# First mixer's attentions: later copies and values, the sink as a column of the softmax rows, one reciprocal for two units

## The reference, cut to what matters

```python
def swa_branch(q, k, v, sinks):            # 6 heads, window of 128, blocks of 128 queries
    scores = einsum(q, k) * (A_DH ** -0.5) # each block of queries against its own block of keys and the one before
    scores = where(valid, scores + alibi, -inf)
    probs = softmax(concatenate([scores, sink], axis=-1), axis=-1)[..., :-1]
    return einsum(probs, v)

def stickbreak_branch(q, k, v):            # 4 heads, blocks of 128 queries against all keys before them
    log_keep = where(strict, log_sigmoid(-z), 0.0)
    suffix = cumsum(log_keep, reverse=True) - log_keep
    a = where(strict, exp(log_sigmoid(z) + suffix), 0.0)
    return einsum(a, v)
```

## Time and profile before

| | us |
|---|---|
| median of three runs | 3040.37 |
| lowest and highest run | 3039.09, 3042.96 |
| profiled execution | 3033.97 |
| its span, first to last instruction | 3032.2 |
| softmax half, from the third pair's scores on (22 pairs) | 58.74 |
| stick half, seven pairs with filled-in products | 38.62 |
| stick half, eight pairs without | 60.54 |
| from the last pair's scores to the barrier | 26.43 |

### The profile page before, as it was taken

The page is one execution under the profiler, slowest core; times in us unless marked ns, Lnnn a source line. Parts: engine busy times, 40 slices in busy tenths (PEclk is TensorE's granted clock), DMA queues, the critical chain, the costliest instruction groups (busy, mean ns, idle before and its releaser), DMA issues.

```text
span 3032.2 us, 39599 instructions
## 1 busy us (share of the span) xinstructions
PE 2841.1 (94%) x15451; PEld 2339.6 (77%) x15451; DVE 2033.7 (67%) x3470; ACT 1163.3 (38%) x1969; POOL 82.3 (3%) x152
## 2 busy tenths in 40 slices
PE   3999999688999998899999999989989999999999
PEld 3878885466888887678888888868757788888887
DVE  5444317768445556558777778779985877777875
ACT  3234227534225555434333334431134433333444
POOL 1000000210130000000000000000000000000000
PEclk7999999898998999799999999999989999999999
DMA  8110200024100000223333274311101333335632
GB/s 310 29 32 22 63 28 10 5 85 126 42 18 1 1 1 1 91 97 111 112 111 111 84 282 142 97 48 47 36 16 63 105 112 111 111 111 194 217 96 102
DMA packets 185700, 256.28 MB, mean 85 GB/s; under 512 B 29575, under 2 KB 138539, under 8 KB 181035
## 3 DMA queue, kind: packets, MB, share of 16 engines
q1 hardware_dynamic: 181520, 232.45, 23.3%
q10 hardware_dynamic: 3995, 21.30, 1.7%
HBM read 186.62 MB, written 67.11 MB: 84 GB/s over the span
## 4 chain that ended last, share of the span: by engine, by line
PE 67%; DVE 8%; ACT 1%; issue 1%; DMA 0%; DVEq 0%; ACTq 0%
PE ps L1567 27%; PE ps L1575 14%; PE ps L1522 10%; PE ps L1470 4%; PE ps L1380 3%; PE ps L1452 2%; PE ps L1434 2%; PE ps L1631 2%; PE ps L1122 1%; PE ps L1682 1%; PE ps L1001 1%; PE ps L1668 0%; DVE ht L2836 0%; PE ps L1358 0%; PE ps L1428 0%
## 5 line engine op out<-in xcount | busy, mean ns | idle before, releaser
L1567 PE MATMUL ps<-x_ops,w_ring 128*128 128x512 f32 x3696 | 840.3, 389 | 6.3 <-ACT even_rows L2185 3.2
L1567 PEld LDWEIGHTS ps<-x_ops,w_ring 128*128 128x128 f32 x3696 | 693.1, 188 | 151.6 <-issue 7.9
L1575 PE MATMUL ps<-a_ring,w_ring 128*128 128x512 f32 x1848 | 419.7, 389 | 0.0
L1575 PEld LDWEIGHTS ps<-a_ring,w_ring 128*128 128x128 f32 x1848 | 346.7, 188 | 72.6 <-DVE w_ring L2925 0.7
L1522 PE MATMUL ps<-h_high,ring_parts 128*128 128x512 f32 x1024 | 320.6, 394 | 18.0 <-DVE h_low L2409 9.3
L2127 ACT ACTIVATE w_ring<-ring 128x512 fp32r<-128x512 f32 x230 | 144.2, 629 | 300.6 <-PE ps L1567 284.8
L1522 PEld LDWEIGHTS ps<-h_high,ring_parts 128*128 128x128 f32 x1024 | 193.5, 190 | 63.7 <-issue 13.5
L2418 DVE TENSOR_TENSOR ring_parts<-ring,ring_parts 128x1024 fp32r<-128x1024 f32 (+2 forms) x77 | 91.7, 1192 | 210.1 <-ACT ring_parts L1769 209.5
L1522 PE MATMUL ps<-h_low,ring_parts 128*128 128x512 f32 x512 | 200.7, 392 | 0.0
L2925 DVE TENSOR_TENSOR w_ring<-ring,w_ring 128x512 fp32r<-128x512 f32 x230 | 157.6, 685 | 38.8 <-ACT w_ring L2127 38.8
L1769 ACT ACTIVATE ring_parts<-ring 128x1024 fp32r<-128x1024 f32 (+2 forms) x77 | 76.0, 989 | 275.7 <-PE ps L1522 177.2
(11 more groups left out here) (476 smaller groups left out, 4637.2 us busy)
## 6 DMA issues: line engine op xcount, KB each, us to landing
a_raw<-act_kept SPq DMA_DIRECT2D x70, 512.0 KB, 3.8
act_kept<-even_rows SPq DMA_DIRECT2D x12, 1536.0 KB, 5.1
act_kept<-odd_rows SPq DMA_DIRECT2D x10, 1536.0 KB, 5.1
ring<-in_ffn_w_gate_dram SPq DMA_DIRECT2D x12, 1024.0 KB, 5.8
ring<-in_ffn_w_up_dram SPq DMA_DIRECT2D x12, 1024.0 KB, 6.0
ring<-in_conv_w_pw_dram SPq DMA_DIRECT2D x24, 512.0 KB, 3.9
late<-in_ffn_w_gate_dram SPq DMA_DIRECT2D x10, 1024.0 KB, 5.8
late<-in_ffn_w_up_dram SPq DMA_DIRECT2D x10, 1024.0 KB, 6.1
```

The costliest lines, as they stand in the source:

```text
L1567: last = mm(o, w_ring[:, i % 4, wp_, P * k:P * k + P], x_ops[:, X_OP[p], rp_, k, :], start=p in "176" and k == 0 and p_ == 0, stop=k == 3 ...
L1575: last = mm(bank(OUT_BANK[DOWN_GROUP[p] + c_]), w_ring[:, (A_UNITS + b) % 4, wp_, P * c_:P * c_ + P], a_ring[:, b % 4, rp_, :], start=p in ...
```

## The change

It touches the one stage. (1) The softmax rows get an input place of their own (`soft_in`, six rows of 260 columns, one per head in the units' order) and an output place (`soft_out`, eight rows). Column 256 of an input row holds the head's sink, negated, written once ahead of the loop. The exponential reads 257 columns and its sum has the sink in it; the sink's own exponential and DVE's sum go. (2) DVE finishes two units at once: after the biases of n and n+1 it waits for the exponentials of n-2 and n-1, takes one reciprocal of two columns and multiplies two rows. (3) `TURN_LAG` becomes `COPY_LAG` = 3 on ACT, and on PE the step of n has the transposes of n-3, the values of n-6 and n-5, and the transposes of n-2. (4) The wait for a free row goes from the biases and, for units 48 and 49, from the sigmoids; `row_freed` is n-3 from unit 52 on and 47 for units 50 and 51.

```diff
-        soft_rows = part(14336, (4 * S,))
+        soft_in = part(14336, (A_H, 260))
+        soft_out = part(14336 + A_H * 260, (8, 260))
...
-        TURN_LAG, OUT_LAG = 4, 7
+        COPY_LAG, VALUE_LAG, OUT_LAG = 3, 6, 7
...
-                return soft_rows[:, 256 * (n % 16):256 * (n % 16) + 256]
+                return soft_out[:, n % 8, 256 - first_units[n].w:256]
...
-            if n < N_SWA:
-                return n - 15
-            return N_SWA - 16 + 4 * (n - N_SWA + 1) if n < N_SWA + 4 else n - 3
+            return n - 3 if n >= N_SWA + 4 else N_SWA - 1
...
-            for n in range(0, N_FIRST + TURN_LAG + 2, 2):
+            for n in range(0, N_FIRST + VALUE_LAG, 2):
                 if n < N_FIRST:
                     scores_pair(n)
                 for m in range(ym_at(n), min(3 * 2 * KC, ym_at(n + 2))):
                     first_parts(m)
-                m = n - TURN_LAG
-                if 0 <= m < N_FIRST:
-                    turned(m)
-                if m >= 2:
-                    values_pair(m - 2)
-                if 0 <= m < N_FIRST:
-                    turned(m + 1)
+                if 0 <= n - 3 < N_FIRST:
+                    turned(n - 3)
+                if n >= VALUE_LAG:
+                    values_pair(n - VALUE_LAG)
+                if 0 <= n - 2 < N_FIRST:
+                    turned(n - 2)
...
-                row = weights_row(n)[:, 0:un.w]
-                f(r[:, 3:4], misc[:, 2 + un.h:3 + un.h], ACT.Exp, bias=r[:, 0:1])
-                f(row, row, ACT.Exp, bias=r[:, 0:1], scale=-1.0, accum_out=r[:, 1:2]).then_inc(s.exp_done, 1)
+                f(soft_out[:, n % 8, 256 - un.w:257], soft_in[:, n % A_H, 256 - un.w:257], ACT.Exp, bias=r[:, 0:1], scale=-1.0,
+                  accum_out=r[:, 1:2]).then_inc(s.exp_done, 1)
...
-                a.wait_ge(s.pt_done, row_freed(n))
+                if n >= N_SWA + 2:
+                    a.wait_ge(s.pt_done, row_freed(n))
...
-            for n in range(N_FIRST + TURN_LAG):
+            for n in range(N_FIRST + COPY_LAG):
...
-                if n >= TURN_LAG:
-                    copy_pt(n - TURN_LAG)
+                if n >= COPY_LAG:
+                    copy_pt(n - COPY_LAG)
...
             def divided(n):
-                un, r = first_units[n], stat[:, n % 16, :]
-                row = weights_row(n)[:, 0:un.w]
-                v.wait_ge(s.exp_done, n + 1)
-                chain(tt(r[:, 1:2], r[:, 1:2], r[:, 3:4], add))
-                chain(v.reciprocal(r[:, 2:3], r[:, 1:2]))
-                ts(row, row, r[:, 2:3], None, mul).then_inc(s.e_done, 1)
+                v.wait_ge(s.exp_done, n + 2)
+                r = stat[:, n % 16:n % 16 + 2, :]
+                chain(v.reciprocal(r[:, :, 2:3], r[:, :, 1:2]))
+                for m in (n, n + 1):
+                    row = weights_row(m)
+                    ts(row, row, stat[:, m % 16, 2:3], None, mul).then_inc(s.e_done, 1)
...
-                if n >= 16:
-                    v.wait_ge(s.pt_done, row_freed(n))
...
-                v.tensor_tensor_reduce(weights_row(n)[:, 0:un.w], un.dist, ps[:, scores_at(n):scores_at(n) + un.w],
+                v.tensor_tensor_reduce(soft_in[:, n % A_H, 256 - un.w:256], un.dist, ps[:, scores_at(n):scores_at(n) + un.w],
...
+            chain(v.tensor_copy(soft_in[:, :, 256:257].rearrange("p (a two) o -> p a (two o)", two=2),
+                                misc[:, 56:62].rearrange("p (two a) -> p a two", two=2)))
             for n in range(N_FIRST + OUT_LAG):
                 if n < N_SWA:
                     soft_biases(n)
-                if 1 <= n <= N_SWA:
-                    divided(n - 1)
+                if n <= N_SWA and n % 2 == (n < N_SWA) and n > 1:
+                    divided(n - 2 - n % 2)
```

## The result

The changed kernel takes 3018.64 us (median; 3011.15 to 3020.09), the kernel before beside it 3040.22 (3039.09 to 3042.96): a ratio of 0.9924, interval 0.9906 to 0.9941. Faster by 21.6 us; 3017.4 was predicted, with 3007 to 3033 as the range.

What follows compares the result with a forecast made beforehand. PE was taken to bound the softmax half and a PE-ACT chain the stick half. Terms 2.2 - 4 - 14 - 7 = -22.8, about -23 us off the median 3040.37, gave 3017.4; range 3007 to 3033.

Steps and rivals of the forecast that it cites:

- The chain named from the earlier trace: Stick half: PE and ACT wait on each other, sigmoids standing behind transposes; 8.98 us per step at width 768.
- the wait of 44.1 us: Stick half: the first sigmoid's wait for PE's transposes would fall from 44.1 us to under 15.
- Softmax half: Softmax part of the attention stage: 2.2 us longer, between -0.5 and +5, from dividing after the pair.
- counted at nothing: Softmax part: 14 us off DVE and 9.6 off ACT win no time, since PE hides both.
- steps without cover: Softmax part: six block_out steps lose 1.2 us, two without a product 0.4, two with weight splits 0.6.
- Seven steps: Stick half, seven steps with products: sigmoids leave the chain, -4 us from 38.62, between -2.5 and -6.
- Eight steps: Stick half, eight steps at widths 512 to 1024: 60.54 us falls to 46.5, -14; bounds -16.9 and -8.8.
- End: From the last scores to the barrier: 26.43 us falls to 19.5, -7, between -4.4 and -9.5.
- 1 (low clock stays): Stick half: PE still waits and keeps the low clock, only -13.5 us in all, 3027; chance 0.21.
- 2 (wait for stick weights): Stick half: sigmoids wait for stick weights instead of transposes, leaving only +2.2 us, 3042.6; chance 0.10.
- 3 (lighter engines show): Softmax part: PE is not the bound, so lighter ACT and DVE win 9.6 us, 3005.6; chance 0.04.
- 4 (softmax half at 1.2 GHz): Softmax part: PE waits inside each step and its clock falls, +47 us there, net +24, 3064; chance 0.05.

Runs made afterwards that it cites:

- experiment 1: The kernel before with only the new order on PE and the copy lag of three: 3018.11 us, ratio 0.9931.
- sink alone: The changed kernel with PE's order and the copy lag of before; sink column, separate rows, paired reciprocals and the division's new place stay: 3037.68 us, ratio 0.9989.
- experiment 4: The kernel before, filled with idle PE products ahead of stick scores: 3030.68 us; with transposes as fillers instead, 3031.59 us.

## Why the prediction was right, and where its terms were off

- **The cause** was right. The chain named from the earlier trace rows is gone, and the order with the lags carries the whole gain (experiment 1). Of the marks it set, the wait of 44.1 us, the steps at 768 (5.51 and 6.11), the block_out steps and the sink's missing gain came out so; the clock, of which it wanted more than 0.95, passed that in the seven steps and stayed at 0.93 and 0.92 behind them.
- **Softmax half**: +2.2 predicted, +1.85 measured, most of it step by step (block_out +0.18 for 0.2, no product +0.18 for 0.2 at 44 and 46, one weight split +0.30; the other, step 6, went the other way, -0.18). But it is a sum of two parts that I had sized wrongly, and that it comes out so near is luck: the relief of DVE and ACT, "counted at nothing", is -3.0 (sink alone), and the new order on PE, whose transposes now wait for the division behind both biases, costs 4.85 on top of it (60.59 against 55.74). Neither does it alone: the new order costs nothing with the division in its old place (58.82), and the division's new place costs nothing that shows under the old order (55.74). In the steps without cover, which the prediction listed for the cost, DVE was the bound before as well, and there the relief counts. "PE is the bound" holds for the steps with a product and nothing else.
- **Seven steps**: -4 predicted, -6.15 measured, just past the upper end. The chain was sized well: from the filled kernel's 37.15 to 32.47 it is 4.7. The clock (1.5 us, nearly all of it in one step, which went from 8.02 to 6.42) was left to the upper end and belonged in the sum.
- **Eight steps**: -14 predicted, -12.2 measured. The 46.5 that I took is what the order gives at full clock (46.67 and 46.99 in two kernels at 1.00, 46.74 in one at 0.96). After ran more of its last step at 1.2 GHz: the scores of width 1024 there took 3.49 us, and the step 8.16 where those three had 6.93 or 6.94.

```profile
593.33 3.49 PE L1276 MATMUL ps<-sk,sq 64*128 64x512 f32 x8 [1.58 <-ACT big L1948]
```

  "What is late next is DVE" holds; part of it is POOL's masks, which the prediction took from the earlier trace rows as they were before, in a DVE that had time. With masks of one column the steps take 44.2, with masks on PE 43.1, close to the 43.6 of the bare chain. (The small end is mis-added: four scores that stay slow are 4 x 1.44 = 5.8 us and not 5.2, so -8.3 for -8.8.)
- **End**: -7 predicted, -6.2 measured. The same two reasons are likely, clock and masks, but not taken apart here; with PE's mask and 2.4 GHz it is 18.67, where "everything at the high clock" had been put at 16.9.
- **The total** fits better than its terms deserve, by luck: -22.8 against -22.7, since two terms erred one way and two the other.
- **The rivals.** 1 (low clock stays) fell, but its subject was nearly half of the gain: had the clock stayed, by experiment 4 the chain's 12 to 13 us would have been left, near its -13.5. 2 (wait for stick weights) fell: 0.2 us. 3 (lighter engines show) is true in size 3.0, not 9.6, and only under the old order on PE. 4 (softmax half at 1.2 GHz) fell: 1.00 in every kernel here.

## What to carry to other kernels

When PE waits inside a chain, price the clock as a term of its own: fill the gap with idle products, and see what the old order takes at full clock. An operation moved on one engine is paid where its cover was thin, so list the steps without cover, and ask for each who was the bound there before. The right lag can change inside a loop: here with the width, at the point where two places for a buffer become one.

## What was not expected of the hardware

- A select on POOL that meets an operation of DVE with two SBUF inputs (product, scan, weight split) and starts during it ends only with it, or up to 0.15 us behind: 2.36 us for two masks that take 0.6 alone, one held up by a scan and one by a product, and 1.04 us for a select of one column that takes 0.19 alone. A mask that becomes ready sooner can so become slower.
- A product of one SBUF input contends too: masks that start with it go through and it takes some 0.09 us longer, masks that start later wait for its end (8 and 7 cases in one trace).
- A weight split's step of the softmax half (32) reacts to every edit out of proportion: 2.97 to 3.84 us over the kernels; the cause was not looked into.
